# Adding the experts' down bias to the residual once, and moving the last tile's gates behind the first up projection

## The chip, the cores and the metric

The kernel runs on one core of a Trainium2 chip. The metric is the device time of one execution in microseconds (us). A core has a matrix engine (TensorE, "PE" in the profile, with its weight loads as "PEld"), a vector engine (VectorE, "DVE"), a scalar engine (ScalarE, "ACT"), GpSimd ("POOL") and SyncE ("SP"), which here only issues DMAs. Each engine works through its own queue in program order; semaphores join the queues. Sixteen DMA engines move data for all of them.

## The reference, cut to what matters

The kernel computes one decoder block for 512 tokens of width 1024: norm, two attention mixers, output projection, residual, and then a mixture of 32 experts of which each token takes four. Only the last part is touched. In the reference it is

```
logits = (xt @ router_w + router_b)
top_v, top_i = lax.top_k(logits, TOP_K)
gate = softmax(top_v)
...
hc = xb @ w1[e] + b1[e]
gt = minimum(hc[:, :D_FF], 7);  up = clip(hc[:, D_FF:], -7, 7)
glu = gt * sigmoid(1.702 * gt)
y = ((up + 1.0) * glu) @ w2[e] + b2[e]        # b2: the down bias
out[token] += gate * y                        # for the token's four experts
```

so that a token's share of the down biases is the sum over its four experts of gate times `b2[e]`: one product of the 512 x 32 matrix of gates with the 32 x 1024 matrix of biases.

## The kernel before

**Stages.** Until about 479 us the core computes norm, projections and attention. From 479 to 549 us the output projection runs in eight half tiles (four token tiles of 128 rows, `NT`, two halves of 512 columns); between them `add_x` adds each half to the residual `xs`, and the router works tile by tile: `choose` picks four experts, `shift`, an exponential on ScalarE and `weigh` make the gates (stored as three half-precision pieces in `value`), `place` and `mark` make one-hot matrices, and `fill_table` multiplies them into a table in PSUM banks 0 and 1. For each expert it has 96 slots (`CAP`) with token number and three gate pieces. The last tile's one-hots come in three parts (`HOT_PARTS`). `take_table` turns the token numbers into gather indices; `fill_gates` then adds the last tile's gate pieces to the same table, and `take_gates` joins them into slot gates (`row_of`), which `spread_rows` and `after_first` spread over 128 rows for the scatter. `after_first` also counts experts with more than 96 tokens (`many`, `extra`).

**Experts.** Expert `e` runs in `expert(e, ...)` and `second(e, ...)`. Weights come as 12 slabs of 1 MB: eight (`w1`) for the up projection and four (`w2`) for the down one, each with one place in the buffer `ring`. On TensorE the order is `up(e)`, `turn_x(e+1)` (transposes of the next gathered rows), `down(e-1)`, `turn_act(e)`, `up(e+1)`. `up` starts with four small bf16 matmuls that put the up bias (L1556), then eight slabs of 12 matmuls (L1562). `down` starts with eight bf16 matmuls that put the down bias into PSUM banks 4 and 5 (L1569, L1572), then four slabs (L1580, L1584). f32 matmuls leave two records each. The biases lie in `bias` as three bf16 pieces stacked over 96 rows; `split_bias` makes them. GpSimd copies one-hot columns for each expert (`picked` into `pick_up`, `pick_down`), gathers the expert's rows from the normed copy `table_d` in HBM two experts ahead (`gathered`), and adds the results to the residual copy `x2_d` in HBM (`scattered`, two indirect DMAs). `store_x2(t)` on SyncE writes `x2_d` first, one tile of 512 KB at a time.

**What sets the order.** Everything is written out by hand. SyncE loads a slab again as soon as TensorE has used it: `load_w1(e+1)` while `up(e)` runs, `load_w2(e)` while `down(e-1)` runs, each slab behind a wait on `w1_used` or `w2_used`. So the ring holds just one expert's weights, and a slab asked for when expert `e` frees its place is wanted again one expert later. The indirect DMAs go through another queue to the same 16 DMA engines.

## Time and profile before

| | |
|---|---|
| median of 3 runs | 1676.53 us (1675.32 to 1678.14) |
| the profiled execution | 1675.77 us |
| its span, first to last instruction | 1674.0 us |
| PE busy | 1591.8 us, 95% |
| DVE, ACT, POOL busy | 440.9, 259.8, 233.9 us |
| chain of work that ended last | PE 88%, DVE 5%, ACT 3%, issue 2%, DMA 1% |
| weight slabs (SyncE's queue) | 384 of 1 MB, median 19.8 us from issue to landing |
| bytes moved | 472.35 MB, 282 GB/s over the span |

Between the span and the run's own time lie 1.77 us. Read the table as the average of stages with different limits: up to 549 us DMA is lightly used, and from about 568 us to the end both TensorE and the 16 DMA engines show 90% or more in nearly every slice. The page gives the slices; the trace gives, for each DMA issue, the time to its landing, and that is the number to follow here.

### The profile page before, as it was taken

The numbers are of one execution on the slowest core, as the hardware profiler recorded it, in microseconds if no ns is written. First come the engines' busy times: TensorE is split into PE (matmuls) and PEld (weight loads), VectorE is DVE, ScalarE is ACT, GpSimd is POOL, SyncE is SP. The second block draws the span as 40 slices with busy tenths as digits, with TensorE's granted clock in tenths as the row PEclk, the third lists the DMA queues.
The fourth block names the chain that finished last, engine by engine and source line by source line (L and its number), as shares of the span: only waits on it lengthen the run. The fifth ranks groups of instructions, "written<-read, shape, count | busy, mean of one in ns | idle before, by whom it ended". The sixth has DMA issues, their size and how long they took to land.

```text
span 1674.0 us, 32752 instructions
## 1 busy us (share of the span) xinstructions
PE 1591.8 (95%) x13380; PEld 645.9 (39%) x13381; DVE 440.9 (26%) x966; ACT 259.8 (16%) x541; POOL 233.9 (14%) x377
## 2 busy tenths in 40 slices
PE   5999999999999789999999999999999999999992
PEld 2654555565445323333333333333333333333331
DVE  4012555332325422113111311131112111211222
ACT  3212444323322100000000000000000000000002
POOL 1000000522200101111111111111111111121101
PEclk8999999999999799999999999999999999999996
DMA  8023120431251789999999999999999999999995
GB/s 224 1 54 73 38 76 13 136 88 51 65 200 51 275 342 376 388 393 386 396 386 395 392 399 386 391 394 399 389 396 399 401 389 394 400 402 390 400 383 177
DMA packets 150302, 472.35 MB, mean 282 GB/s; under 512 B 30537, under 2 KB 71497, under 8 KB 117458
## 3 DMA queue, kind: packets, MB, share of 16 engines
q1 hardware_dynamic: 137458, 446.56, 69.1%
q0 software_dynamic: 12800, 25.17, 6.9%
q8 instruction: 31, 0.51, 0.1%
q14 instruction: 13, 0.11, 0.0%
HBM read 452.41 MB, written 19.29 MB: 282 GB/s over the span
## 4 chain that ended last, share of the span: by engine, by line
PE 88%; DVE 5%; ACT 3%; issue 2%; DMA 1%; DVEq 0%; PEld 0%; POOL 0%; ACTq 0%; PEldq 0%; POOLq 0%; SPq 0%
PE ps L1562 40%; PE ps L1580 13%; PE ps L1181 12%; PE ps L1584 7%; PE ps L1510 3%; PE ps L1323 3%; PE ps L1308 2%; PE ps L1595 2%; PE ps L1536 2%; ACT mixT L995 2%; PE ps L1285 1%; ACT mixT L1004 1%; PE ps L1295 1%; DVE ps L1797 1%; PE ps L1556 1%
## 5 line engine op out<-in xcount | busy, mean ns | idle before, releaser
L1562 PE MATMUL ps<-ring,oT_fox 128*32 128x512 f32 x6144 | 668.8, 595 | 0.0
L1562 PEld LDWEIGHTS ps<-ring,oT_fox 128*32 128x32 f32 x6144 | 184.1, 110 | 462.8 <-issue 459.2
L1580 PE MATMUL ps<-ring,hT 128*32 128x512 f32 x2048 | 264.1, 592 | 0.0
L2101 DVE TENSOR_TENSOR mixT<-ps,mask 128x768 f32<-128x768 f32 x64 | 61.1, 954 | 650.2 <-PE ps L1562 650.2
L1584 PE MATMUL ps<-ring,hT 128*32 128x256 f32 x2048 | 154.8, 379 | 0.0
L1323 PE MATMUL ps<-hT,ring 128*128 128x512 f32 x304 | 137.3, 599 | 0.0
L1584 PEld LDWEIGHTS ps<-ring,hT 128*32 128x32 f32 x2048 | 61.3, 110 | 158.4 <-issue 158.4
L1119 ACT ACTIVATE mixT<-mixT 128x768 f32<-128x768 f32 x32 | 27.0, 845 | 609.8 <-DVE mixT L2105 609.8
L1181 PE MATMUL ps<-hT,ring 128*128 128x512 f32 x208 | 93.2, 609 | 7.0 <-ACT hT L929 7.0
L841 POOL COPY pT<-pT 96x32 bf16 (+1 forms) x64 | 13.8, 218 | 575.5 <-ACT hT L1129 566.3
L2130 DVE COPY hT<-ps 128x384 f32<-128x384 f32 x64 | 32.8, 553 | 181.0 <-PE ps L1595 180.9
L1323 PEld LDWEIGHTS ps<-hT,ring 128*128 128x128 f32 x304 | 55.5, 191 | 64.2 <-issue 64.2
L1129 ACT ACTIVATE hT<-ps,v_fox 128x512 f32<-128x512 f32 x64 | 33.7, 577 | 295.9 <-PE ps L1584 295.9
L1580 PEld LDWEIGHTS ps<-ring,hT 128*32 128x32 f32 x2048 | 61.1, 110 | 46.5
L1181 PEld LDWEIGHTS ps<-hT,ring 128*128 128x128 f32 x208 | 40.2, 195 | 56.5 <-issue 56.4
L995 ACT ACTIVATE mixT<-ps,st 128x128 f32<-128x128 f32 (+1 forms) x96 | 49.1, 536 | 78.1 <-DVE st L1803 78.1
L1510 PE MATMUL ps<-ring,mixT 128*128 128x512 f32 x128 | 59.0, 601 | 2.1 <-DVE qk L1930 2.1
L832 POOL DMA_INDIRECT x<-hT,v_win x32 | 50.6, 1580 | 26.2 <-POOL v_win L829 24.5
L834 POOL DMA_INDIRECT x<-hT,v_win x32 | 49.7, 1552 | 9.8 <-issue 9.8
L1181 PEld LDWEIGHTS ps<-ring,hT 128*128 128x128 f32 x384 | 45.2, 192 | 2.3 <-issue 2.3
L1181 PE MATMUL ps<-ring,hT 128*128 128x128 f32 (+1 forms) x384 | 45.5, 279 | 0.0
L818 POOL COPY v_win<-v_win 96x1 int32 (+1 forms) x30 | 5.9, 196 | 259.4 <-DMA x<-hT,v_win 231.0
(291 smaller groups left out, 1162.4 us busy)
## 6 DMA issues: line engine op xcount, KB each, us to landing
ring<-in_expert_w SPq DMA_DIRECT2D x384, 1024.0 KB, 19.8
ring<-in_w_in SPq DMA_DIRECT2D x28, 512.0 KB, 4.8
ring<-in_w_out SPq DMA_DIRECT2D x8, 512.0 KB, 7.6
ring<-in_w_in SPq DMA_DIRECT2D x1, 3168.0 KB, 12.9
xs<-in_x SPq DMA_DIRECT2D x4, 512.0 KB, 5.1
ring<-in_w_in SPq DMA_DIRECT2D x8, 256.0 KB, 3.6
ring<-in_w_proj_nsa SPq DMA_DIRECT2D x16, 128.0 KB, 2.9
ring<-in_w_proj_fox SPq DMA_DIRECT2D x8, 256.0 KB, 3.3
```

The source lines that it names most:

```text
L832: pool.indirect_dma_start(out=x2_half, out_offset=bass.IndirectOffsetOnAxis(ap=now_half[b], axis=0), in_=yb[b][:, 0:512], in_offset=None, ...
L834: pool.indirect_dma_start(out=x2_quarter, out_offset=bass.IndirectOffsetOnAxis(ap=now_quarter[b], axis=0), in_=yb[b][:, 512:768], in_offse ...
L995: last = act.activation(probs[:, h, P_OFF[t]:P_OFF[t] + P * (t + 1)], scores(h, t), ACT.Exp, bias=ngm[:, h, t:t + 1], accum_out=sums[:, h, ...
L1129: ins = act.activation(yb[b][:, cols], y_ps[:, cols], ACT.Copy, scale=gate)
L1181: last = pe.matmul(dst, lhs(c), rhs(c), start=(c == 0), stop=(c == n - 1))
L1308: ins = pe.matmul(o_bank[h * DH:(h + 1) * DH, kt * P:S], v[:, kt, h * DH:(h + 1) * DH], pT[:, h, at:at + S - kt * P], start=(first and n = ...
L1323: ins = pe.matmul(w, w_c(c), hT[:, c, :], start=(c == 0), stop=(c == NK - 1))
L1510: ins = pe.matmul(ps[:, u, :], mixT[:, k, t * P:(t + 1) * P], w_o[k][:, n * 512:(n + 1) * 512], start=(k == 0), stop=(k == NK - 1))
L1562: ins = pe.matmul(wide(ps[TG * j:TG * j + TG, g, :]), xT[b][:, c, TG * g:TG * g + TG], up_slab(c, j), start=(c == 0), stop=(c == NK - 1), ...
L1580: pe.matmul(ps[TG * q:TG * q + TG, 4, :], gT[b][:, 2 * (q // 2) + h, TG * j:TG * j + TG], ring[:, NK + j, at:at + 512], start=False, stop= ...
L1584: ins = pe.matmul(ps[TG * q:TG * q + TG, 5, 0:256], gT[b][:, 4 + h, TG * j:TG * j + TG], ring[:, NK + j, at:at + 256], start=False, stop=( ...
L2101: return dve.tensor_tensor(to, half, b_up[:, 256 * n:256 * n + 256].unsqueeze(1).broadcast_to([P, NG, 256]), ALU.add)
```

## The change

- The down bias leaves the experts. `down` puts none; `pick_down` and its copies on GpSimd go, and `split_bias` makes pieces of the up bias alone.
- In its place the biases are loaded as f32 into `rope_cos` and `rope_sin`, four copies of 32 rows each (eight DMAs of 64 KB, issued before the projection of the mixers). `give_b_down(k)`, for k from 0 to 3, multiplies transposed gates by them, two matmuls of 32 rows by 128 columns over 512 columns each, after the slabs 4 to 7 of `up(1)`; VectorE adds each 128 x 512 result to `xs`, eight additions.
- `xs` is complete only then. The four `x2_d` stores move from the router's stage (three there, one after the first gather) to SyncE's queue between `load_w1(2)` and `load_w2(1)`. GpSimd's wait for them stands where it stood, ahead of `block(1)`; `down(0)` waits for the last addition, since banks 4 and 5 hold the products.
- `fill_gates` writes to a part of bank 5 of its own and runs after `turn_x(1)`, inside `expert(0)`, with four matmuls more that transpose the gates and one that clears. `take_gates` and `after_first` come after `expert(0)` on VectorE, `spread_rows` after slab 2 of `up(1)`; the count of overfull experts (`count_extra`) comes ahead of `expert(0)`. `take_parts` saves the table.

```diff
@@ b_raw, b_mid, bias, pick_up
-        b_raw = [ring_f[0:E, 0:2 * F], hT_f[0:E, 0:D]]
+        b_raw = ring_f[0:E, 0:2 * F]
+        b_down = [rope_cos, rope_sin]
+        gates_T = pcT[:, 0:P]
@@ SyncE
-            sp.dma_start(b_raw[1], expert_b2[0]).then_inc(b_loaded, 16)
+            for n in range(2):
+                for t in range(NT):
+                    sp.dma_start(b_down[n][E * t:E * (t + 1), :], expert_b2[0][:, n * 512:(n + 1) * 512]).then_inc(b_loaded, 16)
...
             for t in range(NT - 1):
-                store_x2(t)
                 store_table(t)
...
             sp.wait_ge(xg_loaded[0], 16)
-            store_x2(NT - 1)
...
             load_w1(1)
-            with sp.Fori(1, E - 1) as e:
+            load_w1(2)
+            sp.wait_ge(x2_ready, 4 * NT)
+            for t in range(NT):
+                sp.dma_start(x2_d[1 + t * P:1 + (t + 1) * P, :], xs[:, t, :]).then_inc(x2_stored, 16)
+            load_w2(1)
+            with sp.Fori(2, E - 1) as e:
@@ GpSimd
             picked(pick_up, 0, 0, pick_up_ready)
-            for b in range(2):
-                picked(pick_down, b, b, pick_down_ready)
-            pool.wait_ge(idx_ready, 6)
+            pool.wait_ge(idx_ready, 2)
...
             block(0, 0, True, 0)
             pool.wait_ge(x2_stored, 16 * (NT + 1))
+            pool.wait_ge(idx_ready, 6)
@@ TensorE
             def fill_gates():
                 pe.wait_ge(gates_ready, NT)
+                for t in range(NT):
+                    pe.matmul(ps[E * t:E * (t + 1), 4, 0:P], expd[:, t, :], ident[:, :], start=True, stop=True,
+                              tile_position=(0, E * t))
...
-            pe.wait_ge(idx_ready, 2)
-            fill_gates()
...
             def down(b, loaded, used):
-                for q in range(4):
-                    n = q % 2
-                    pe.matmul(ps[TG * q:TG * q + TG, 4, :], pick_down[:, b, :], bias[:, 2 * F + n * 512:2 * F + (n + 1) * 512],
-                              start=True, stop=False, tile_position=(0, TG * q))
-                for q in range(4):
-                    pe.matmul(ps[TG * q:TG * q + TG, 5, 0:256], pick_down[:, b, :], bias[:, 2 * F + q * 256:2 * F + (q + 1) * 256],
-                              start=True, stop=False, tile_position=(0, TG * q))
...
+            def give_b_down(k):
+                if k == 0:
+                    pe.wait_ge(idx_ready, 6)
+                    pe.wait_ge(b_loaded, 16 * (2 * NT + 1))
+                else:
+                    pe.wait_ge(x2_ready, 2 * NT + 2 * k)
+                for m in range(2):
+                    t = 2 * (k % 2) + m
+                    rows = slice(E * t, E * (t + 1))
+                    pe.matmul(ps[:, 4 + m, :], gates_T[rows, :], b_down[k // 2][rows, :], start=True, stop=True,
+                              tile_position=(E * t, 0)).then_inc(b_down_full, 1)
...
+                    if isinstance(e, int) and e == 1 and c >= 4:
+                        give_b_down(c - 4)
+                    if isinstance(e, int) and e == 1 and c == 2:
+                        pe.wait_ge(rows_ready, 1)
+                        spread_rows(4, 0, 2 * E, row_of.rearrange("p v e -> p (v e)")).then_inc(table_full, 1)
...
+                if not before:
+                    fill_gates()
...
-                pe.wait_ge(pick_down_ready, e + 1)
+                else:
+                    pe.wait_ge(x2_ready, 4 * NT)
@@ VectorE
+                for k in range(4):
+                    for m in range(2):
+                        t, n = 2 * (k % 2) + m, k // 2
+                        dve.wait_ge(b_down_full, 2 * k + m + 1)
+                        sl = xs[:, t, n * 512:(n + 1) * 512]
+                        dve.tensor_tensor(sl, sl, ps[:, 4 + m, :], ALU.add).then_inc(x2_ready, 1)
...
             take_x(0, 0)
+            count_extra()
+            expert(0, 0, True)
+            take_gates()
             after_first()
-            expert(0, 0, True)
```

SyncE's queue after the last tile's table store (`table<-hT`; `x<-xs` is a store to `x2_d`, `ring<-in_expert_w` a slab, 2x1024 wide for `w2`). Before:

```order
L615 DMA table<-hT 128x1024 [waits x_normed]
L619 DMA x<-xs 128x1024 [waits x2_ready,xg_loaded0]
L611 DMA ring<-in_expert_w 128x2x1024 x4
L611 DMA ring<-in_expert_w 128x2048 [waits w1_used] x8
L650 UNCONDITIONAL_BRANCH
```

and changed:

```order
L622 DMA table<-hT 128x1024 [waits x_normed]
L618 DMA ring<-in_expert_w 128x2x1024 [waits xg_loaded0]
L618 DMA ring<-in_expert_w 128x2x1024 x3
L618 DMA ring<-in_expert_w 128x2048 [waits w1_used] x16
L654 DMA x<-xs 128x1024 [waits x2_ready]
L654 DMA x<-xs 128x1024 x3
L618 DMA ring<-in_expert_w 128x2x1024 [waits w2_used] x4
L656 UNCONDITIONAL_BRANCH
```

All four stores now stand behind the slabs that `up(1)` frees and ahead of those that `down(0)` frees.

TensorE from the last one-hot part to the first slab of expert 0 (`ident,oT_nsa` is `turn_x`, `v_fox,ident` is `spread_rows`, `pT` the up bias). Before:

```order
L1495 MATMUL ps<-v_sel,qk 96x3 [waits gates_ready,idx_ready]
L1495 MATMUL ps<-v_sel,qk 96x3 x31
L1536 MATMUL ps<-ident,oT_nsa 128x96 [waits rows_ready,xg_loaded0,consts2,bias_ready]
L1536 MATMUL ps<-ident,oT_nsa 128x96 x7
L1503 MATMUL ps<-v_fox,ident 32x64 x8
L1556 MATMUL ps<-pT 32x512 [waits pick_up_ready,xT_ready]
L1556 MATMUL ps<-pT 32x512 x3
L1562 MATMUL ps<-ring,oT_fox 32x512 [waits slab_loaded0]
```

and changed:

```order
L1538 MATMUL ps<-ident,oT_nsa 128x96 [waits idx_ready,xg_loaded0,consts2,bias_ready]
L1538 MATMUL ps<-ident,oT_nsa 128x96 x7
L1558 MATMUL ps<-pT 32x512 [waits parts_taken,pick_up_ready,xT_ready]
L1558 MATMUL ps<-pT 32x512 x3
L1564 MATMUL ps<-ring,oT_fox 32x512 [waits slab_loaded0]
```

`turn_x(0)` no longer waits for `rows_ready`; the gather (`xg_loaded0`) stays.

TensorE from slab 6 of `up(1)` to `down(0)` (`rope_sin,pcT` is `give_b_down`). Before:

```order
L1562 MATMUL ps<-ring,oT_fox 32x512 [waits slab_loaded6]
L1562 MATMUL ps<-ring,oT_fox 32x512 x11
L1562 MATMUL ps<-ring,oT_fox 32x512 [waits slab_loaded7]
L1562 MATMUL ps<-ring,oT_fox 32x512 x11
L1536 MATMUL ps<-ident,oT_nsa 128x96 [waits gT_ready,xg_loaded0]
L1536 MATMUL ps<-ident,oT_nsa 128x96 x7
L1569 MATMUL ps<-pT 32x512 [waits pick_down_ready,gT_ready]
L1569 MATMUL ps<-pT 32x512 x3
L1572 MATMUL ps<-pT 32x256 x4
L1580 MATMUL ps<-ring,hT 32x512 [waits slab_loaded8]
```

and changed:

```order
L1564 MATMUL ps<-ring,oT_fox 32x512 [waits slab_loaded6]
L1564 MATMUL ps<-ring,oT_fox 32x512 x11
L1607 MATMUL ps<-rope_sin,pcT 128x512 [waits x2_ready]
L1607 MATMUL ps<-rope_sin,pcT 128x512
L1564 MATMUL ps<-ring,oT_fox 32x512 [waits slab_loaded7]
L1564 MATMUL ps<-ring,oT_fox 32x512 x11
L1607 MATMUL ps<-rope_sin,pcT 128x512 [waits x2_ready]
L1607 MATMUL ps<-rope_sin,pcT 128x512
L1538 MATMUL ps<-ident,oT_nsa 128x96 [waits gT_ready,xg_loaded0]
L1538 MATMUL ps<-ident,oT_nsa 128x96 x7
L1575 MATMUL ps<-ring,hT 32x512 [waits slab_loaded8,x2_ready,gT_ready]
```

The eight bias matmuls at the head of `down` are gone, for this and every other expert; pairs of new ones stand between the slabs of `up(1)` alone, and `down(0)` waits for the additions.

## Rows read from the trace of the kernel before

**Rows 1.** TensorE's timeline over one expert: start, length (us), line, count.

```profile
668.18 20.77 PE L1562 MATMUL ps<-ring,oT_fox 128*32 128x512 f32 x192
...
689.70 0.40 PE L1569 MATMUL ps<-pT 96*32 96x512 bf16 x4
...
690.03 1.03 PE L1580 MATMUL ps<-ring,hT 128*32 128x512 f32 x8
...
701.49 20.77 PE L1562 MATMUL ps<-ring,oT_fox 128*32 128x512 f32 x192
```

**Rows 2.** Slab loads, five singly, then all: issue (ns), start and landing (us).

```profile
L611 SPq DMA_DIRECT2D ring<-in_expert_w x1: 333/333/333, 622.6 to 622.6; - x1
...
DMA to landing us min/median/max: 6.1/6.1/6.1
...
L611 SPq DMA_DIRECT2D ring<-in_expert_w x1: 349/349/349, 637.9 to 637.9; - x1
...
DMA to landing us min/median/max: 7.9/7.9/7.9
...
L611 SPq DMA_DIRECT2D ring<-in_expert_w x1: 4060/4060/4060, 1137.5 to 1137.5; - x1
...
DMA to landing us min/median/max: 22.9/22.9/22.9
...
L611 SPq DMA_DIRECT2D ring<-in_expert_w x1: 3864/3864/3864, 1544.2 to 1544.2; - x1
...
DMA to landing us min/median/max: 21.5/21.5/21.5
...
L611 SPq DMA_DIRECT2D ring<-in_expert_w x1: 3457/3457/3457, 1554.7 to 1554.7; - x1
...
  PEld ps L1562: 0.3, 1
...
DMA to landing us min/median/max: 27.8/27.8/27.8
...
DMA to landing us min/median/max: 4.8/19.8/29.9
```

**Rows 3.** Stretches: us, busy time by engine, PE clock, DMA share, GB/s.

```profile
494.50:498.80 4.30, 4.30 (x14) 2.10 (x13) 1.51 (x6) 2.42 (x4) 0.58 (x1) 1.00 0.30 122
600.00:604.00 4.00, 4.00 (x24) 0.85 (x20) 0.00 (x0) 0.00 (x0) 0.00 (x0) 0.56 0.17 58
624.00:640.00 16.00, 16.00 (x186) 5.68 (x178) 5.37 (x9) 2.50 (x4) 3.64 (x5) 1.00 0.95 342
```

**Rows 4.** DMA queues, 1360 to 1460 us: packets, MB, share of 16 engines.

```profile
q1 hardware_dynamic: 6647, 37.26, 92.2%
q0 software_dynamic: 1200, 2.36, 10.6%
```

**Rows 5.** Timeline of all engines from the last residual addition to `turn_x(0)`.

```profile
548.71 0.69 DVE L1943 TENSOR_TENSOR xs<-xs,ps 128x512 f32<-128x512 f32 x1 [3.74 <-PE ps L1510]
...
561.62 2.69 PE L1495 MATMUL ps<-v_sel,qk 128*96 128x3 f16 x32 [0.96 <-DVE v_win L2007]
563.41 0.33 SPq L619 DMA_DIRECT2D x<-xs  x1
...
566.09 1.51 PE L1536 MATMUL ps<-ident,oT_nsa 96*128 96x96 f32 x8 [1.78 <-DVE v_fox L2011]
```

**Rows 6.** Timeline of all engines between the first two up projections.

```profile
592.58 0.61 POOL L818 COPY v_win<-v_win 96x1 int32 x1 [21.37 <-PE ps L1536]
...
594.93 0.23 POOL L841 COPY pT<-pT 96x32 bf16 x1
...
597.78 1.51 PE L1595 MATMUL ps<-ident,mixT 128*128 128x128 f32 x6 [5.46 <-DVE mixT L2127]
...
599.62 22.72 PE L1562 MATMUL ps<-ring,oT_fox 128*32 128x512 f32 x192
```

**Rows 7.** The score matmuls' (L1285) own busy time in a stretch.

```profile
167.00:169.60 2.60, 2.43 (x16) 1.69 (x16) 1.00 0.00 0
```

More of the change, by code:

```diff
@@ L437, in hybrid_block @@
         rows_ready = sem("rows_ready")
+        parts_taken = sem("parts_taken")
         bias_hi = sem("bias_hi")
@@ L1584, in down @@
                         ins = pe.matmul(ps[TG * q:TG * q + TG, 5, 0:256], gT[b][:, 4 + h, TG * j:TG * j + TG],
-                                        ring[:, NK + j, at:at + 256], start=False, stop=(c == NK - 1),
+                                        ring[:, NK + j, at:at + 256], start=(c == 0), stop=(c == NK - 1),
                                         tile_position=(0, TG * q))
@@ L2016, in valid_row, with take_parts @@
                 yield dve.tensor_tensor(to, pad, v, ALU.add)
+            def take_parts():
+                step.link(dve.tensor_copy(split[:, HOT_PARTS[0][1]:, :], table_of(HOT_PARTS[0][1], E)))
+                step.link(dve.tensor_copy(split[:, 0:HOT_PARTS[0][1], :], table_of(0, HOT_PARTS[0][1])))
+                dve.sem_inc(parts_taken, 1)
             def take_gates():
                 dve.wait_ge(table_full, NT + 3)
-                for first, end in ((0, HOT_PARTS[0][1]), (HOT_PARTS[0][1], E)):
-                    step.link(dve.tensor_copy(split[:, first:end, :], table_of(first, end)))
+                step.link(dve.tensor_copy(gates_T, ps[:, 4, 0:P]))
+                step.link(dve.tensor_tensor(split[:, :, 1:4], split[:, :, 1:4], late_of(0, E), ALU.add))
                 for ins in valid_row(row_of[:, 0, :], split[:, :, 0], row_pad):
@@ L2055, in _ @@
             step.link(dve.tensor_copy(count, routed(NT - 1, 2)))
+            take_table(1)
+            take_parts()
             weigh(NT - 1)
-            take_table(1)
-            take_gates()
             def slot_rows(to_half, to_quarter, halves_, quarters_, signal):
```

74 lines of the change are left out of this document (34 added, 40 removed).

## The prediction

> **What bounds the kernel now.** I read the slices of the page first: from about 568 us on TensorE is busy and its clock is full, so a TensorE-bound kernel is the first guess. Its timeline over one expert confirms the pace [rows 1]: `up(3)` begins at 668.18 and `up(4)` at 701.49, 33.31 us apart, and an up projection takes 20.77 us, 2.6 us for a slab. No wait stands between.
>
> But DMA is as busy. In 100 us of this stretch the slab loads take 92.2% of the 16 engines and the indirect DMAs 10.6% [rows 4]: full, at 37.26 + 2.36 MB or 396 GB/s. Whether DMA keeps up is told by the time from issue to landing [rows 2]. The slab asked for at 637.9 (the first of expert 3) lands after 7.9 us, the same slab of expert 18, asked for at 1137.5, after 22.9, and the last but one of expert 30's up slabs, asked for at 1554.7, after 27.8. So a queue builds up: TensorE asks for 12 slabs in 33.31 us, and DMA delivers them in more. From landing to landing, expert 3 to 18: (1160.4 - 645.8) / 15 = 34.31 us. Expert 18 to 30 (1544.2 + 21.5 = 1565.7): (1565.7 - 1160.4) / 12 = 33.78 us. A ring of one expert's weights can lend about 30 us, and it has lent them all: at 1554.7 + 27.8 = 1582.5 a weight load of TensorE waited 0.3 us for exactly that slab [rows 2]. TensorE reached its matmuls at 1567.5 (668.18 plus 27 periods) + 6 x 2.59 = 1583.0. So the slack, wide at first, ends at about 0.5 us just before the end. **The kernel before is TensorE-bound by half a microsecond, with DMA behind it.** What TensorE saves is worth at most that, until the last slabs of expert 30 have come; what DMA is given to carry is what to count.
>
> **What TensorE saves and pays.** (a) The head of `down`: from 689.70 to 690.03 the matmuls of the down bias hold it for 0.34 us [rows 1] (their records are longer but overlap). 32 x 0.34 = 10.9 us go, with nothing beside them on TensorE. (b) The start of expert 0: `turn_x(0)` begins at 566.09, after `fill_gates` (561.62, 2.69 us) and VectorE's `take_gates` [rows 5]. Without them the gather is late next: SyncE, which waits for it too, goes on at 563.41. So it can begin near 563.45, 2.6 us earlier, and not more. `take_parts` and `weigh` on VectorE, some 2.7 us after the last one-hot, are done before the transposes are. (c) `fill_gates` goes into a hole: between `turn_x(1)` and `turn_act(0)` TensorE is idle for 5.46 us [rows 6], while VectorE and ScalarE work on expert 0. It took 2.69 us at half clock, and with five matmuls more stays under 4 at either clock, so it costs nothing. (d) Of the clock: from 599.62 `up(1)` takes 22.72 us instead of 20.77, since the clock fell to 1.2 GHz in the hole (mean 0.56 between 600 and 604, [rows 3]). With the hole half filled the clock either stays at 2.4 GHz, 2.0 us gained, or falls again, nothing gained; I call it even.
> (e) Inside `up(1)`: the spread is 8 small f32 matmuls, nearest to the eight turning ones (1.51 us at half clock, [rows 5]), 0.4 at least, 0.8 at most at full. The eight matmuls of `give_b_down` have 512 columns of f32. Twelve of up's, four abreast, take 2.59 us, so one alone takes 0.86. A pair uses different rows of the array. The score matmuls, two heads on 64 rows each, show what that does: 8 matmuls with 2560 columns, 4.3 us one after the other, take 2.43 us [rows 7]. So a pair takes 0.86 to 1.73 us; I take 0.97, since only the scores have this form: four pairs 3.9 us (3.5 to 6.9). The waits in them are covered: two additions of 0.69 us [rows 5] lie under the 2.6 us of the next slab. After the last pair they are not: 1.5 us, of which `turn_x(2)` covers 0.8, leaves 0.7 before `down(0)`.
> The chapter on packing small matmuls in the Trainium skill (TensorE: Matmul & The Clock Gate, Part 3) states that tiles on different row groups run concurrently and that four with 32 rows gained 3.07 times; by it a pair would cost 0.9, which the scores' row supports for two groups.
>
> TensorE alone would thus end 10.9 + 2.6 - 0.4 - 3.9 - 0.7 = 8.5 us earlier, 10.5 with the clock kept.
>
> **What DMA is given.** (f) The four stores to `x2_d` were spread over the router's stage, where DMA is a third busy: one store, alone between 494.5 and 498.8, is 0.30 of 4.3 us, 1.3 us of all 16 engines [rows 3]. Now they are issued near 623 us, four times 1.3 = 5.2 us. (g) GpSimd waits for them ahead of `block(1)`. Behind that wait stand the gather for expert 3, the pick of expert 2's up bias and the first scatter. The gather ran near 594 [rows 6], and DMA was at 0.17 from 600 to 604 [rows 3]; now it comes after 631. The indirect DMAs of an expert cost 10.6 / 3 = 3.5 us [rows 4], a gather between a third and a half: 1.2 (to 1.8). (h) What the queue can use: from 624 to 640 DMA was at 0.95, 0.8 us idle [rows 3]. (i) When the queue starts. Since it stands nearly still at 600, it starts when `up(1)` frees its first slab. That is 2.6 us earlier from (b), 4.6 with the clock kept; the spread and three pairs delay the last slab by 3.3. So that slab, asked for at 622.6 and landed at 628.7 [rows 2], is asked for at 621.3. With 3.6 us from one slab to the next no queue is left then, and it lands after the least that any load took, 4.8 us [rows 2]: at 626.1, 2.6 us earlier than before, or 0.6 if the clock falls. The stores follow within 2.5 us of its request, so DMA does not stand still between.
> Sum of f to i at `w1(3)`: 5.2 + 1.2 - 0.8 - 2.6 = **3.0 us later** (5.0 if the clock falls). `up(2)` starts as before or 2 us later.
>
> **From there to the end.** TensorE's period is now 33.31 - 0.34 = 32.97, and the landing time grows by 34.31 - 32.97 = 1.34 us an expert, from 7.9 + 3.0 = 10.9 at expert 3. There is one thing to gain. DMA was faster, 33.78 instead of 34.31, from the point on at which a slab took 22.9 us to land; there an issue, before 0.35 us long, took SyncE 4.06 us [rows 2], so the queue was full. If the rate goes with the full queue (what the rows suggest and do not prove), it comes after (22.9 - 10.9) / 1.34 = 9 experts, at 12 instead of 18: 6 x 0.53 = 3.2 us gained. Slab 6 of expert 30 then lands -0.2 us (clock kept) to +1.8 us against before. TensorE, up to some 8 us early, will have run into the queue near expert 20 and takes it at landing. The end, against the profiled execution: the slack of 0.5 goes, and three `down`s after it are shorter by 1.0: -1.5 - 0.2 = -1.7 us, or -1.5 + 1.8 = +0.3. The middle is -0.7 us on 1675.77: 1675.1. The median of the runs is 0.76 above that execution, so 1675.8 us.
> The pages DMA: Bandwidth & Descriptors (Bandwidth) and HBM Reference (Specifications) of the Trainium skill give 425 GB/s for a core streaming alone. At that rate an expert's data would take 31 us, DMA would stay ahead and the first rival below would hold; the 396 GB/s of rows 4, with all engines occupied, speak against it for this mix of loads and scatters.
>
> **Rivals.**
> *TensorE's gain arrives.* If DMA speeds up under more pressure, as it did once by 1.5%, to 33 us an expert, the end follows TensorE: 1675.77 - 8.5 or - 10.5, on the median 1666 to 1668. It needs 0.8 us an expert more than any stretch showed. 0.1.
> *No quickening.* The faster rate belongs to something else (the late experts' addresses, say) and does not come sooner: +3.2, on the median 1678.0 with the clock kept, 1680.0 without. 0.28.
> *Slower: the stores and the gather in the full queue.* The stores and the gather are simply more for a full queue: without quickening, with the clock falling, a pair at 1.73 (three of them, +2.3 before the last slab is freed) and a gather at 1.8, it is 5.0 + 2.3 + 0.6 - 1.5 = +6.4, on the median 1683. It is slower by over 0.2% from the point at which slab 6 of expert 30 lands 4.9 us later than before. 0.1, beside the slow end of the case above.
> *A stall from the stores.* `up(2)` needs its pick, 2.6 us after GpSimd's wait ends (592.58 to 595.16, [rows 6]). The stores land near 631, the pick comes at 633.6, `up(2)` starts at 668.18 - 33.31 = 634.9. If it is late by 1 or 2 us, TensorE has 20 us of slack in hand at that place: no effect on the end.
> *It does not do what it says* is excluded for the matmuls, which are gone from the program's order.
>
> **How the numbers follow.** The likeliest, DMA-bound with the faster rate sooner, has 0.5 and gives 1675.8, its own range 1673.0 to 1678.5. No quickening 0.28, TensorE's gain 0.1, slower beyond it 0.1, and 0.02 left over. A measurement of this kernel tells 0.2%, 3.4 us, from no change: below 1673.2 is faster, above 1679.9 slower. Faster: 0.1 from the first rival and 0.11 of the likeliest. Same: 0.39 of the likeliest and 0.18 of no quickening. Slower: 0.1 of that, 0.1, and the rest. The range leaves out the gain and the worst of the slower side: 1671 to 1681.
>
> **What the changed profile will show if this is right.** The period of TensorE 32.97 us until about expert 20, then waits of PEld for `ring<-in_expert_w` in nearly every expert, together some 8 us, and a period of 33.7. Slabs near expert 12 landing after 23 us, SyncE's issues getting long from there on rather than from expert 18. `turn_x(0)` at 563.5, `down(0)` near 623.4, stores issued at 623 and landed by 632. Wrong, if no wait for slabs shows (then the first rival), if the landing time starts above 12 us at expert 3 (then the traffic was under-counted), or if the rate near expert 15 is still 34.3.

## The result, and the profile after

The changed kernel takes 1679.01 us (median of 20 runs, 1676.28 to 1681.70) against 1676.64 us (1674.34 to 1678.44, 20 runs): a ratio of 1.0015, with a 95% interval of 1.0009 to 1.0021. It is **slower by 2.4 us** where 0.7 us faster was forecast. It stays inside the stated range of 1671 to 1681 us, but the sign was wrong. Measured once more (e15 below), it gave 1.0014 (1.0005 to 1.0023).

The chain of work that ended last, by engine, now holds 21% of DMA, where before it was 1%:

```profile
PE 68%; DMA 21%; DVE 5%; ACT 3%; issue 2%; DVEq 0%; PEld 0%; SPq 0%; POOL 0%; ACTq 0%; PEldq 0%; POOLq 0%
```

TensorE's timeline over one expert, which answers to rows 1 (start, length in us, line, count):

```profile
672.07 20.77 PE L1564 MATMUL ps<-ring,oT_fox 128*32 128x512 f32 x192
692.78 0.88 PE L1538 MATMUL ps<-ident,oT_nsa 96*128 96x96 f32 x8
693.59 1.07 PE L1575 MATMUL ps<-ring,hT 128*32 128x512 f32 x8
...
705.08 7.47 PE L1564 MATMUL ps<-ring,oT_fox 128*32 128x512 f32 x68
```

The down bias is gone and the period is 705.08 - 672.07 = 33.0 us, as predicted (32.97). The slab loads, which answer to rows 2: slab 7 of expert 2, slab 0 of experts 3 and 12, slab 6 of expert 30 (issue in ns, start, time to landing in us), then who waited for any slab from 1200 us on:

```profile
L618 SPq DMA_DIRECT2D ring<-in_expert_w x1: 328/328/328, 625.1 to 625.1; - x1
...
DMA to landing us min/median/max: 4.7/4.7/4.7
...
L618 SPq DMA_DIRECT2D ring<-in_expert_w x1: 356/356/356, 642.0 to 642.0; - x1
...
DMA to landing us min/median/max: 11.1/11.1/11.1
...
L618 SPq DMA_DIRECT2D ring<-in_expert_w x1: 3186/3186/3186, 939.1 to 939.1; - x1
...
DMA to landing us min/median/max: 22.9/22.9/22.9
...
L618 SPq DMA_DIRECT2D ring<-in_expert_w x1: 953/953/953, 1560.8 to 1560.8; - x1
...
  PEld ps L1564: 0.7, 1
...
DMA to landing us min/median/max: 26.0/26.0/26.0
...
  PEld ps L1564: 19.8, 33
```

Slab 0 of expert 3 lands at 653.1, 7.3 us later than before (645.8, [rows 2]). It took 11.1 us to land, where the sum gave 10.9, but that this fits is luck: it was asked for 4.2 us later and landed 7.3 us later, both more than forecast. At expert 12 a slab takes 22.9 us and the issue 3.2 us, the state that the kernel before reached at expert 18. From about expert 20 TensorE's weight loads wait for slabs (33 waits in up alone; most of each lies beside matmuls that still run, and the period is 33.8). Slab 6 of expert 30 lands at 1586.8 instead of 1582.5. So the course of the queue (the loads asked for and not yet landed) is the one foretold; its start is later than foretold. Where that start is set, in TensorE's timeline of `up(1)` (answers to rows 6):

```profile
596.99 1.51 PE L1590 MATMUL ps<-ident,mixT 128*128 128x128 f32 x6 [3.52 <-DVE mixT L2158]
...
598.83 7.34 PE L1564 MATMUL ps<-ring,oT_fox 128*32 128x512 f32 x52
```

```profile
608.15 0.39 PE L1507 MATMUL ps<-v_fox,ident 96*32 96x64 f32 x16
608.38 5.32 PE L1564 MATMUL ps<-ring,oT_fox 128*32 128x512 f32 x48
613.63 1.13 PE L1607 MATMUL ps<-rope_cos,pcT 32*128 32x512 f32 x4
614.69 2.78 PE L1564 MATMUL ps<-ring,oT_fox 128*32 128x512 f32 x24
617.40 1.13 PE L1607 MATMUL ps<-rope_cos,pcT 32*128 32x512 f32 x4
...
627.48 1.06 PE L1575 MATMUL ps<-ring,hT 128*32 128x512 f32 x8 [0.61 <-issue]
```

A pair holds the slabs up by 617.40 - 613.63 - 2.59 = 1.18 us, the spread by 0.23, and `down(0)` waits 0.6 us for the last additions. The DMA engines before (first fence) and after (second), in stretches: us, busy time by engine, granted clock, DMA share, GB/s:

```profile
600.00:610.00 10.00, 10.00 (x80) 2.45 (x76) 0.00 (x0) 0.60 (x1) 0.00 (x0) 0.82 0.51 181
610.00:620.00 10.00, 10.00 (x96) 2.62 (x92) 0.00 (x0) 0.00 (x0) 0.00 (x0) 1.00 1.00 407
620.00:624.00 4.00, 4.00 (x48) 1.62 (x44) 1.44 (x3) 0.00 (x0) 0.00 (x0) 1.00 1.01 412
```

```profile
600.00:604.00 4.00, 4.00 (x32) 0.94 (x28) 0.53 (x3) 0.60 (x1) 0.00 (x0) 0.75 0.08 33
...
600.00:610.00 10.00, 10.00 (x100) 2.64 (x96) 1.13 (x7) 0.60 (x1) 0.00 (x0) 0.90 0.59 224
610.00:620.00 10.00, 10.00 (x84) 2.62 (x80) 2.57 (x4) 0.00 (x0) 0.00 (x0) 1.00 0.92 354
620.00:624.00 4.00, 4.00 (x36) 1.01 (x32) 1.28 (x2) 0.00 (x0) 0.00 (x0) 1.00 0.73 285
624.00:628.00 4.00, 3.39 (x32) 1.37 (x28) 1.90 (x3) 0.00 (x0) 0.00 (x0) 1.00 0.76 291
...
624.00:640.00 16.00, 15.37 (x174) 7.15 (x170) 8.00 (x12) 1.90 (x3) 1.65 (x5) 1.00 0.95 359
```

With a slab freed every 3.77 us DMA runs dry between slabs just where the kernel before keeps it full. From 624 to 640 us it is at 0.95, as before ([rows 3]): the 0.8 us of idle time there, which the stores were to use, is idle still. And the hole before `turn_act(0)` is still 3.5 us wide, and the clock fell in it as before.

### The profile page after: what moved, and what is told of

Its sections match the earlier page's. It is cut to its first block, busy times and chain, and to the rows that moved or that the text cites. A ratio compares the mean times of both kernels' runs of the same rounds, so it can differ in the third digit from the quotient of the medians.

```text
span 1677.1 us, 32232 instructions
## 1 busy us (share of the span) xinstructions
PE 1588.6 (95%) x13149; PEld 649.4 (39%) x13150; DVE 444.1 (26%) x974; ACT 255.8 (15%) x537; POOL 229.8 (14%) x345
## 4 chain that ended last, share of the span: by engine, by line
PE 68%; DMA 21%; DVE 5%; ACT 3%; issue 2%; DVEq 0%; PEld 0%; SPq 0%; POOL 0%; ACTq 0%; PEldq 0%; POOLq 0%
PE ps L1564 26%; DMA ring<-in_expert_w 20%; PE ps L1180 11%; PE ps L1575 10%; PE ps L1579 5%; PE ps L1514 3%; PE ps L1322 3%; PE ps L1307 2%; ACT mixT L998 1%; PE ps L1284 1%; ACT mixT L1007 1%; PE ps L1294 1%; PE ps L1590 1%; PE ps L1538 1%; DVE ps L1817 1%
## 5 line engine op out<-in xcount | busy, mean ns | idle before, releaser
L1575 PE MATMUL ps<-ring,hT 128*32 128x512 f32 x2048 | 267.7, 594 | 7.3 <-DMA ring<-in_expert_w 5.7
L1579 PEld LDWEIGHTS ps<-ring,hT 128*32 128x32 f32 x2048 | 67.0, 110 | 152.7 <-issue 152.7
L835 POOL COPY v_win<-v_win 128x1 int32 (+1 forms) x64 | 9.7, 183 | 554.2 <-ACT hT L1128 554.2
L1575 PEld LDWEIGHTS ps<-ring,hT 128*32 128x32 f32 x2048 | 61.4, 109 | 54.5 <-DMA ring<-in_expert_w 16.0
L1128 ACT ACTIVATE hT<-ps,v_fox 128x512 f32<-128x512 f32 x64 | 33.6, 577 | 295.0 <-PE ps L1579 295.0
```

Of the source, the lines that this page charges most:

```text
L1128: ins = act.activation(yb[b][:, cols], y_ps[:, cols], ACT.Copy, scale=gate)
L1575: pe.matmul(ps[TG * q:TG * q + TG, 4, :], gT[b][:, 2 * (q // 2) + h, TG * j:TG * j + TG], ring[:, NK + j, at:at + 512], start=(c == 0), st ...
L1579: ins = pe.matmul(ps[TG * q:TG * q + TG, 5, 0:256], gT[b][:, 4 + h, TG * j:TG * j + TG], ring[:, NK + j, at:at + 256], start=(c == 0), sto ...
```

## The experiments

Each run was measured beside the kernel before, on the same chip. "Against before" is the ratio of the times; 0.001 is 1.7 us, and gains in the text are differences of these ratios. e1, e5, e6 and e14 leave the down bias out of the output, and e3 and e4 part of the down weights: they are there to price a part. The times to the right are of the profiled execution: start of `up(0)`, `up(1)` and `up(2)`, slab 7 of expert 2 asked for, slab 0 of expert 3 landed, and from there to the landing of slab 0 of expert 30 (us; "-": the trace has no landings of weight slabs there).

| run | median | against before (95%) | up(0) | up(1) | up(2) | 2.7 asked | 3.0 landed | to 30.0 |
|---|---|---|---|---|---|---|---|---|
| before | 1676.64 | 1 | 568.7 | 599.6 | 634.9 | 622.6 | 645.8 | 919.9 |
| change | 1679.01 | 1.0015 (1.0009-1.0021) | 568.6 | 598.8 | 639.1 | 625.1 | 653.1 | 917.1 |
| e15, change again | 1679.77 | 1.0014 (1.0005-1.0023) | 568.7 | 599.8 | 640.9 | 626.4 | 655.2 | 917.4 |
| e1, stores early | 1676.14 | 0.9999 (0.9991-1.0008) | 567.3 | 597.9 | 638.3 | 624.4 | 647.5 | 918.4 |
| e2, before, late stores | 1683.40 | 1.0043 (1.0030-1.0055) | 570.8 | 600.8 | 639.1 | 623.2 | 652.3 | 923.0 |
| e3, change, 11 MB | 1670.98 | 0.9968 (0.9955-0.9981) | 569.3 | 600.3 | 641.1 | 626.9 | 652.0 | 889.7 |
| e4, before, 11 MB | 1676.32 | 0.9998 (0.9989-1.0007) | 571.5 | 601.4 | 636.1 | 623.8 | 647.3 | 897.7 |
| e5, before, no bias | 1673.66 | 0.9978 (0.9968-0.9988) | 571.1 | 601.9 | 636.7 | 624.7 | 647.9 | 918.4 |
| e6, no pairs | 1678.02 | 1.0011 (1.0002-1.0020) | 567.8 | 599.1 | 639.2 | 622.4 | 652.3 | 918.8 |
| e7, gather first | 1678.23 | 1.0009 (1.0000-1.0018) | 568.0 | 599.3 | 640.0 | 626.1 | 652.3 | 917.9 |
| e14, no pairs, pick first | 1674.52 | 0.9987 (0.9978-0.9996) | 567.8 | 599.0 | 634.3 | 622.2 | 649.9 | 916.2 |
| e13, late stores, pick first | 1678.29 | 1.0013 (1.0004-1.0021) | 570.3 | 600.1 | 634.8 | 622.3 | 650.0 | 917.9 |
| e9, hole filled | 1676.43 | 0.9995 (0.9986-1.0004) | 569.0 | 599.3 | 638.0 | 624.0 | 653.7 | 914.2 |
| e12, before, hole filled | 1674.04 | 0.9985 (0.9976-0.9994) | 570.5 | 599.5 | 632.8 | 620.5 | - | - |
| e8, bias in up(0) | 1673.06 | 0.9977 (0.9968-0.9986) | 569.5 | 603.2 | 637.2 | 625.0 | - | - |
| e10, change, clock kept | 1673.05 | 0.9982 (0.9973-0.9991) | 567.9 | 596.0 | 634.5 | 620.6 | - | - |
| e11, up(0), clock kept | 1669.55 | 0.9955 (0.9942-0.9969) | 569.5 | 600.2 | 633.4 | 621.2 | - | - |

**What is the saving worth alone, and to TensorE alone?** e5 is the kernel before with the eight bias matmuls of `down` (L1569, L1572) deleted. e3 and e4 take DMA out of the way, in the change and in before:

```diff
                     dst = ring[:, c, :].rearrange("p (k n) -> p k n", k=2)
+                    if c >= 10 and not (isinstance(e, int) and e == 0):
+                        dst, src = dst[:, 0, :], src[:, 0, :]
```

> The kernel before without the eight down bias matmuls at the head of down, for all experts; nothing else of the change (the down bias is missing from the output). It does the gain of the change alone, with no traffic moved and no pairs. Theory T1 (DMA ends it): TensorE's period falls to 32.97 us but the end follows DMA: the queue fills some 4 experts earlier (18 to about 14), which gives 1.5 to 2 us, 0.7 us come from down(0) and down(1) at the start and 1.0 us from the last three downs: 2.5 to 3.5 us faster than before. Rival (TensorE's saving arrives whole): 32 x 0.34 = 10.9 us faster. Rival (the rate quickens at a fixed expert, whatever the queue): 1 to 1.5 us faster.

> The changed kernel, but for experts 1 to 31 half of each of the last two down slabs is not loaded (11 MB an expert instead of 12, so the output is wrong from expert 1 on); TensorE does the same work. This takes DMA out of the way and shows what the change is worth to TensorE alone. T1: no queue builds up, TensorE's period is 32.97 us to the end, and the end is 6.5 to 8.5 us ahead of the kernel before. Rival T3 (TensorE's saving is not there, for instance because the down bias was hidden beside the slabs): within 1 us of the run with the same loads on the kernel before.

> The kernel before with the same halves of down slabs left out from expert 1 on (output wrong in the same way). If the kernel before is bound by TensorE with 0.5 us to spare, as read, it keeps its time: 0 to 0.7 us less. If DMA already costs it something through contention or through late slabs that the trace does not show, it gains more than 1 us.

The saving alone gives 3.7 us, a little more than the 2.5 to 3.5 expected and far from 10.9: DMA ends it, as held. e4 keeps its time (0.3 us less, inside its interval), so the kernel before is bound by TensorE; in e3 all 27 experts take 889.7 us from landing to landing, 32.95 each, and it ends 5.3 us ahead of e4. That is TensorE's gain from the whole change: 5.3 (medians; 5.0 by the ratios), not the 8.5 that I summed. `up(2)` begins 5.0 us later in e3 than in e4 although `up(0)` begins 2.2 us earlier. So 3 us of the sum were wrong on TensorE's own side, all before `up(2)`.

**The stores.** e1 puts them back, e2 moves them in the kernel before:

```diff
@@ e1, SyncE (the additions on VectorE wait for x2_stored)
             for t in range(NT - 1):
+                store_x2(t)
                 store_table(t)
...
             sp.wait_ge(xg_loaded[0], 16)
+            store_x2(NT - 1)
...
             load_w1(2)
-            sp.wait_ge(x2_ready, 4 * NT)
-            for t in range(NT):
-                sp.dma_start(x2_d[1 + t * P:1 + (t + 1) * P, :], xs[:, t, :]).then_inc(x2_stored, 16)
@@ e2, SyncE
-                store_x2(t)
                 store_table(t)
...
             sp.wait_ge(xg_loaded[0], 16)
-            store_x2(NT - 1)
...
             load_w1(1)
-            with sp.Fori(1, E - 1) as e:
+            load_w1(2)
+            sp.wait_ge(x2_ready, 2 * NT)
+            for t in range(NT):
+                sp.dma_start(x2_d[1 + t * P:1 + (t + 1) * P, :], xs[:, t, :]).then_inc(x2_stored, 16)
+            load_w2(1)
+            with sp.Fori(2, E - 1) as e:
```

> The changed kernel with the four x2_d stores put back to the router's stage, where they stood before. The additions of the down bias come after them, so the down bias is missing from the output; all else runs as in the changed kernel. Theory T1 (the DMA traffic that the change puts into the full queue decides): slab 0 of expert 3 lands 5 to 7 us earlier than with the change (653.1 there), near 647; the rate then quickens some 4 experts later, which gives back 2 to 2.5 us; the end is 2 to 4 us earlier than with the change, 0 to 1.5 us ahead of the kernel before. Rival T2 (what TensorE does and waits for inside the first two up projections decides: pairs, spread, clock): the same time as the change, 2 to 2.5 us behind the kernel before, and slab 0 of expert 3 within 1.5 us of 653.

> The kernel before with one thing of the change alone: the four x2_d stores moved to SyncE's queue between load_w1(2) and load_w2(1). Down bias and gates stay as they were. T1: slab 0 of expert 3 lands 5 to 6 us later than before (645.8), the quickening comes 4 to 5 experts earlier and gives back 2 to 2.5 us, and the slack of 0.5 us goes: 2 to 3 us slower than before. T2: no difference to before over 0.5 us.

e1 is 2.7 us faster than the change (ratios 0.9999 and 1.0015) and its slab lands at 647.5, as theory T1 has it. e2 has the traffic (652.3) but costs 7 us, more than twice what T1 gave. Its waits of TensorE from 635 to 642 us and its timeline show why (GpSimd's copy that sat idle for the stores, its pick, `up(2)`):

```profile
PE ps L1555 <- POOL pT L840: 3.2, 1, 3.2
```

```profile
636.42 0.18 POOL L817 COPY v_win<-v_win 96x1 int32 x1 [63.09 <-DMA x<-xs]
...
638.34 0.37 POOL L840 COPY pT<-pT 96x32 bf16 x2
...
638.71 0.62 PE L1555 MATMUL ps<-pT 96*32 96x512 bf16 x4 [3.24 <-POOL pT L840]
```

Its clock in three stretches from there on was at 0.74, 0.50 and 0.90:

```profile
636.00:640.00 4.00, 1.29 (x12) 0.46 (x16) 0.20 (x1) 0.00 (x0) 1.94 (x7) 0.74 1.03 422
640.00:644.00 4.00, 4.00 (x24) 0.97 (x20) 0.00 (x0) 0.00 (x0) 2.97 (x2) 0.50 1.02 353
644.00:648.00 4.00, 4.00 (x40) 1.16 (x36) 0.00 (x0) 0.60 (x1) 0.00 (x0) 0.90 1.11 306
```

The stores land late in the queue, the pick of expert 2 stands behind them on GpSimd, TensorE waits 3.2 us, the clock falls, and `up(3)` begins at 675.2 (668.1 in e13, without the stall). This is the stall that the prediction priced at nothing. e13 is e2 with one line of GpSimd moved:

```diff
                     picked(pick_down, e + 1, o, pick_down_ready)
+                    pool.wait_ge(x2_stored, 16 * (NT + 1))
                     now_scatter(e - 1, o)
...
             block(0, 0, True, 0)
-            pool.wait_ge(x2_stored, 16 * (NT + 1))
```

> The kernel before with the late stores (as in the second run of the first set, which was 6.7 us slower than before), and with GpSimd's gather for expert 3 and its picks for expert 2 ahead of the wait for these stores. Output complete. Theory (the stores cost twice there: 2 MB in a full queue, and up(2), whose pick stood behind GpSimd's wait for them, 3.2 us late and then 6.8 us at 1.2 GHz): up(2) starts on time, the clock stays, up(3) begins 5 to 6 us earlier than in that run, and what is left is the traffic: 2 to 3.5 us slower than before. Rival (it is all traffic, the stall is hidden by slack): 5.5 to 7 us slower than before, as without this edit.

1.0013 instead of 1.0043: 5 us were the stall, 2.2 us the traffic. In the change itself `up(2)` just escapes: the pick was there at 638.70 and the first matmul at 638.84; in e15 TensorE waited 0.5 us for it.

**The gather** (the same move of GpSimd's wait in the change, e7):

> The changed kernel with GpSimd's gather for expert 3 and its pick for expert 2 ahead of the wait for the x2_d stores instead of behind it (output complete). T1: the gather runs near 594 us, when DMA is nearly idle, instead of in the full queue: slab 0 of expert 3 lands 1.2 us earlier, of which the later quickening takes 0.4 back: 0.5 to 1.2 us faster than the change. If up(2) waits for that pick (it came 0.14 us before up(2)'s first matmul in the changed kernel), some executions gain 1 to 3 us more and the spread of the times becomes smaller. Rival: the gather costs nothing there, same time within 0.3 us.

1.0 us by the ratios, inside the expectation and not separable from zero by the intervals; the slab lands 0.8 us and 2.9 us earlier than in the two profiles of the change.

**The pairs.** e6 is the change without `give_b_down` and without the additions; e14 is e6 with GpSimd's move of e7.

```diff
-                    if isinstance(e, int) and e == 1 and c >= 4:
-                        give_b_down(c - 4)
+                    if isinstance(e, int) and e == 1 and c == 4:
+                        pe.wait_ge(idx_ready, 6)
```

> The changed kernel without the eight matmuls of give_b_down and the eight additions (the down bias is missing from the output); the stores stay behind load_w1(2). Three pairs stand before the last slab that up(1) frees. If a pair costs 1.18 us there, as the slab periods of the changed kernel show (3.77 against 2.59 us), slab 7 of expert 2 is asked for 3.5 us earlier, slab 0 of expert 3 lands 3 to 4 us earlier (near 649.5), the quickening comes 2 to 3 experts later and gives 1.2 to 1.6 us back: 1.5 to 2.5 us faster than the change. Rival (the traffic alone counts, when TensorE frees a slab does not, since a queue stands anyway): within 0.5 us of the change.

> The changed kernel without the pairs and additions (down bias missing from the output), with GpSimd's gather for expert 3 and pick for expert 2 ahead of the wait for the stores. Against the run with the gather first and the pairs in place (1.2 us slower than before) it tells what the pairs cost without the stall of up(2) that spoiled the earlier run without pairs. Theory: without pairs DMA is not idle between the slabs of up(1) (0.6 MB, 1.5 us) : 1 to 2 us faster than that run, within 0.7 us of before. Rival (the pairs cost TensorE 5 us, and TensorE's position counts): 3.5 to 5 us faster than that run. Rival (nothing of the pairs reaches the end): within 0.4 us of it.

e6 gained only 0.7 us, and it decides nothing: with TensorE earlier, `up(2)` waited 4.4 us for its pick.

```profile
PE ps L1558 <- POOL pT L847: 4.4, 1, 4.4
```

Without that stall (e14) the pairs' absence gives 3.7 us against e7, which is the rival's number and twice mine. `up(1)` to `up(2)` takes 35.3 us in e14 and 40.7 in e7: the pairs and the wait behind them cost TensorE 5.4 us, not 4.6. And without them DMA is kept full from 610 to 624 us:

```profile
610.00:620.00 10.00, 10.00 (x100) 2.61 (x96) 0.00 (x0) 0.00 (x0) 0.00 (x0) 1.00 0.98 396
620.00:624.00 4.00, 4.00 (x44) 1.52 (x40) 1.69 (x3) 0.14 (x1) 0.00 (x0) 1.00 1.05 397
```

That is 396 and 397 GB/s, against 354 and 285 in the change. I had expected 1.5 us from the idle DMA and the later quickening to take part of it back. It took nothing: e14 asks for slab 0 of expert 3 at 637.3, 5.7 us earlier than e7, and gets it only 2.4 us earlier, so its queue is the deeper one (12.6 us to landing against 9.3) and the faster rate comes sooner, not later. e14 takes away two things at once, the idle DMA and TensorE's 5.4 us; what each of them costs at the end is not separated.

**The clock.** Five matmuls that nobody reads fill the hole before `turn_act(0)` in the change (e9), seven in the kernel before (e12):

```diff
                 if not before:
                     fill_gates()
+                    pe.wait_ge(b_loaded, 16 * (2 * NT + 1))
+                    for _ in range(5):
+                        pe.matmul(ps[:, 4, P:4 * P], ident[:, :], b_down[0][:, P:4 * P], start=True, stop=True)
```

> The changed kernel with five more f32 matmuls of 384 columns (3.2 us at full clock) right behind fill_gates, into a part of bank 4 that nobody reads; the output is complete. They fill the hole before turn_act(0) that the change left 3.5 us wide. Theory: TensorE is then without a pause of more than 0.5 us there, the granted clock stays at 2.4 GHz from 571 us on instead of falling near 595 for 6.8 us, up(1) takes 2.0 us less in the stretch 598 to 602, and the end is 1.0 to 2.0 us ahead of the change. Rival: the clock falls whatever stands in the hole: 0 to 0.5 us slower than the change. If DMA sets when slab 0 of expert 3 lands whatever TensorE's clock does, up(1) is 2 us shorter and the end stays.

> The kernel before with seven such matmuls of 384 columns (into bank 5, read by nobody) between turn_x(1) and turn_act(0), where TensorE is idle for 5.5 us. Output complete. It tells what the clock's fall at 596.7 us costs a kernel that TensorE bounds: the fall gone, up(1) 1.7 to 2.0 us shorter, all slabs from expert 2 on asked for 2 us earlier; the slack at expert 30 stays as it is, and the end is 1.5 to 2.0 us faster than before. Rival (DMA sets the end whatever TensorE does from here): 0 to 0.5 us faster.

The stretch from 594 to 604 us in the change, then in e9 (granted clock third from the end):

```profile
594.00:604.00 10.00, 7.01 (x46) 2.60 (x50) 5.25 (x12) 0.60 (x1) 0.00 (x0) 0.66 0.60 247
```

```profile
594.00:604.00 10.00, 9.81 (x82) 4.53 (x84) 6.30 (x14) 1.15 (x2) 0.00 (x0) 1.00 0.70 270
```

A mean of 0.66 is 6.8 of 10 us at 1.2 GHz. The clock fell there in each of the seven profiles with the change's hole and in each of the six with a wider or similar one, and in none of the four with such matmuls. e9 is 3.3 us faster than the change, e12 2.5 us faster than before; `up(1)` to `up(2)` takes 38.7 us in e9, where the change had 40.2 and e15, with its wait of 0.5 us, 41.2; and 33.3 in e12 instead of 35.3. Each gives somewhat more than the 1.6 to 2.0 us of the stretch, and more than I expected. In e9 that is a faster queue (914.2 us to expert 30, slab 0 of expert 3 no earlier), which I can't explain fully.
The page TensorE: Matmul & The Clock Gate (Why this matters for your kernels) of the Trainium skill says that idle gaps between bursts of matmuls are to be avoided, because the clock drops back after them; e9 and e12 agree, with 1.00 from 594 to 604 us where the change and the kernel before had 0.66.

**A version that beats both.** e8 computes the same as the change with the product in `up(0)`, four matmuls on four row groups at once after slabs 3 and 5, the stores between `load_w1(1)` and `load_w1(2)`, and the gather first. e10 is e7 with matmuls in TensorE's waits at the hole and between 554 us and `turn_x(0)`; e11 is e8 with those.

```diff
@@ e8, TensorE (up(0)) and SyncE
+                    if not before and c == 1:
+                        turn_gates()
+                    if not before and c in (3, 5):
+                        give_b_down((c - 3) // 2)
...
             load_w1(1)
-            load_w1(2)
             sp.wait_ge(x2_ready, 4 * NT)
             for t in range(NT):
                 sp.dma_start(x2_d[1 + t * P:1 + (t + 1) * P, :], xs[:, t, :]).then_inc(x2_stored, 16)
+            load_w1(2)
@@ e10 and e11, TensorE (keep_busy: as many f32 matmuls of 384 columns)
             route(2 * NT - 1)
+            pe.wait_ge(b_loaded, 16 * (2 * NT + 1))
+            keep_busy(3)
             count_earlier(NT - 1)
             for part in range(len(HOT_PARTS)):
+                if part < 2:
+                    keep_busy(1 + part)
                 fill_table(NT - 1, part)
+            keep_busy(4)
```

> The same computation as the changed kernel, with the same removals from down, but what the change puts into up(1) stands in up(0): the gates are transposed after slab 1, and after slabs 3 and 5 four matmuls of give_b_down on four row groups at once; VectorE adds during up(0); the four x2_d stores go between load_w1(1) and load_w1(2), and GpSimd's gather for expert 3 ahead of its wait for them. Theory (two things made the change slower: the stores in a full queue, and the pairs that leave DMA idle between the slabs of up(1)): the stores fill the hole that DMA has at 600 to 606 us (share 0.17 to 0.6), up(1) has no pairs, slab 0 of expert 3 lands within 1.5 us of where the kernel before has it (645.8 to 647.3), and the end is 0 to 2.5 us faster than before, 2.5 to 5 us faster than the change. If only the stores counted: as the run with the stores early, 0 to 0.5 us faster than before. If the product of gates and biases costs DMA or TensorE the same wherever it stands: within 1 us of the change.

> The changed kernel with the gather first and with matmuls that nobody reads (128 x 128 by 384 columns of f32) in TensorE's waits: five behind fill_gates as before, and ten between the last router matmuls at 554 us and turn_x(0). Output complete. Theory (at the two places the clock falls because TensorE waits, and it costs up(0) and up(1) at 1.2 GHz): the granted clock stays at 2.4 GHz from the output projection to the last expert; up(0) begins 0.5 to 1.5 us earlier and takes 1.5 to 2.5 us less, up(1) 2 us less; all slabs are asked for 4 us earlier, of which the later quickening takes 1 to 1.5 back: 3.5 to 6 us faster than the change, 1 to 4 us faster than before. Rival (the clock falls there whatever TensorE does): 0.5 to 3 us faster than the change, from the hole alone.

> The kernel with the down bias in up(0) and the stores behind load_w1(1), with the same matmuls in TensorE's waits as the run above. Output complete. If the two causes (traffic and idle DMA on one side, the clock on the other) add up, it is 3 to 6 us faster than before; if what one gives is taken back by the queue's later quickening, 2 to 3 us.

e8 gives 0.9977, 3.9 us faster than before and more than expected: as much as the saving alone (e5, 0.9978), so the rest of the change (the earlier `up(0)` on one side, product, stores and gates on the other) comes to nothing at the end. Which of e8's edits does it, the product's place, its four row groups, the stores' place or the gather, is not separated. From 600 to 604 us its DMA engines are full with the stores, where those of the change had 0.08 ([rows 3] had 0.17):

```profile
600.00:604.00 4.00, 2.65 (x14) 1.49 (x18) 2.76 (x7) 0.00 (x0) 0.00 (x0) 0.50 1.00 411
```

e10 gives 0.9982, 5.5 us less than the change, as expected, and e11 0.9955: **7.5 us faster than before** (7.1 by the medians), more than expected. The two causes add up nearly: the extra matmuls give 4.5 us on e7 (e10) and 3.7 us on e8 (e11). In e10 the clock stood at 0.89 from 556 to 572 us, where the change had 0.52, and from `up(0)` to `up(1)` it took 28.0 us instead of 30.2:

```profile
594.00:604.00 10.00, 9.81 (x105) 3.39 (x107) 3.18 (x9) 0.60 (x1) 0.00 (x0) 1.00 1.01 371
556.00:572.00 16.00, 13.76 (x106) 7.04 (x110) 11.58 (x32) 1.46 (x3) 5.04 (x6) 0.89 0.67 242
```

The trace of e11 has TensorE waiting for slabs as often as that of the change (34 times in `up`, 36 in the change), so DMA still ends it.

**The change again.**

> The changed kernel once more, unedited, for a second profiled execution. In the first one all of TensorE's work up to 556 us came 2.6 us late because of where the clock had fallen early in the execution. If that was chance, this execution has another lead or lag there (up(0) from 566 to 569.5 us), and what lies between up(0) and slab 0 of expert 3 (84.5 us in the first) is the same within 1 us; the median is 2 to 3 us above the kernel before.

The median is 2.4 to 2.8 us above before both times. `up(0)` begins at 568.6 and 568.7. The kernels with the start of before begin it at 570.3 to 571.5, except the profiled execution of before itself, at 568.7: that one was ahead of its kind by some 2 us, not the change behind by 2.6. From `up(0)` to the landing it was 84.5 and 86.5 us, 2 us apart where I expected 1, so the last 1 or 2 us of a sum made from single traces are chance.

## Why the prediction was wrong, step by step

Means of profiled executions: of the runs with the start and `up(1)` of before (before, e2, e4, e5, e13) and of those with the start and pairs of the change (the change twice, e1, e3, e7).

- **(a), and what bounds the kernel before: right.** Period 33.0; e4 shows TensorE as the limit, e5 DMA close behind it. The half microsecond itself is read from one trace, and both fit it.
- **(b), half wrong.** `up(0)` begins 568.4 instead of 570.5, 2.1 us earlier (2.6 predicted; the gather was late next, as said: `turn_x(0)` waited 2.8 us for it). But `up(1)` begins only 1.5 us earlier (599.2, 600.8). The time won lies in a stretch at 1.2 GHz, which ended at 572.3 us instead of 573.3, only about 1 us earlier: the same work took 30.8 us instead of 30.3.
- **(c), right:** `fill_gates` is hidden. **(d), the step that failed first.** I called the clock even and took the middle. It fell in all seven profiles that have this hole, in which 3.5 us without a matmul were left. That alone is 1.0 us of the forecast, and the case with the clock falling stood at +0.3. With the clock kept (e9) the sum stood at -1.7, and e9 measured -0.8 (-2.3 to +0.7). So the clock was worth 3.3 us at the end, where the sum had 2.0.
- **(e), mis-sized.** A pair 1.18 us instead of 0.97, additions as said, spread 0.23. Over `up(1)` to `up(2)` the change adds 5.7 us (40.6, 35.0; e2 with its stall left out, e5 counted with the 0.34 us that it saves) where the sum gave 4.7.
- **(f), (g), right:** stores 6.7 us between e1 and the mean of the change, 1.3 of it e1's earlier start, so 5.4 (5.2 predicted); the gather about 1 (1.2 predicted). **(h), wrong:** the 0.8 us of idle DMA from 624 to 640 us were not used, the share there is 0.95 as before, 0.93 in e15. From the landing of slab 7 of expert 2 to that of slab 0 of expert 3 the change takes 6.7 us more (23.4, 16.7), where f, g and h gave 5.6.
- **(i), the term that turned the sign.** Slab 7 of expert 2 was to be asked for 1.3 us earlier, or 0.7 later with the clock falling. It was 2.5 us later (625.8, 623.3): (b), (d) and (e) all come together here, since it is TensorE that frees the slab and DMA is idle until it does. It landed 0.4 us later than before (630.8, 630.3), not 2.6 or 0.6 us earlier; that it lands 4.8 us after it is asked for held (4.7 and 5.3 us). So the sum at slab 0 of expert 3 was +3.0 or +5.0 and the two profiles have 654.2 against 647.0 (before, e4, e5): **+7.2**.
- **The quickening, right.** A slab took 22.9 us to land at expert 12, as forecast. From slab 0 of expert 3 to that of expert 30 the change took 917.1 and 917.4 us, before 919.9: 2.7 us gained (3.2 predicted). With the prediction's 34.31 us an expert up to the point at which a slab takes 22.9 us, and 33.78 after it, the same rule gives 918.2 for e5 (measured 918.4), 918.7 for e1 (918.4), 917.9 for e13 (917.9) and 915.7 for e14 (916.2). It misses e2 (919.7 against 923.0) and e9 (916.2 against 914.2). The rule holds for sums, but it is no clean step: in the change the experts up to 13 come at 33.9 to 34.2 us, but three of them at 34.7 to 35.2, and 33.8 is reached at expert 14; in e13 the issues take 2.7 to 6.9 us from expert 12 on and the rate is 34.0 until expert 18. "No quickening" falls: an expert settled near 33.8 us (33.6 to 34.0) from expert 19 on in the kernel before, from 14 on in the change and from 13 on in e14, so the faster rate does not belong to fixed experts.
- **The end.** +7.2 - 2.7 - 1.5 = +3.0 us; the medians say +2.4 and +2.8. What bounds the kernel, and the quickening, held; the error is the 2.2 to 4.2 us at the queue's start: 1.0 to 3.0 of it at slab 7 of expert 2, by (b), (d) and (e), and 1.1 behind it, most of it (h).
- **The stall, priced at nothing, was wrong in its reason.** "20 us of slack in hand" is the time that a slab waits for TensorE, not time that TensorE can lose: a kernel bound by TensorE with 0.5 us to spare pays every stall (e2, e6). In the change it missed by 0.1 us, and in e15 TensorE waited 0.5 us.

## What to carry to other kernels

When two engines are nearly level, sum a change at the point where the second one's queue begins, and ask there when each buffer is freed: work put between the last buffers freed left DMA idle here, while the same work one stage earlier, where the loader is ahead, cost nothing at the end (e8). A fall of the clock belongs into the sum wherever a wait like those of this case is left (3.2 us in e2, 3.5 in the change, 4.4 in e6, 5.5 before); filling the wait with matmuls is worth trying even on an engine that is short of time. Move a wait on one engine only after looking at what small steps stand behind it in its queue.

## What was not expected of the hardware

A pair of f32 matmuls with 32 rows and 512 columns on two row groups took 1.06 us between two slabs (613.63 to 614.69), and four on four row groups took 1.07 us in e8:

```profile
582.31 1.14 PE L1604 MATMUL ps<-rope_cos,pcT 32*128 32x512 f32 x8
583.38 5.36 PE L1562 MATMUL ps<-ring,oT_fox 128*32 128x512 f32 x48
588.66 1.14 PE L1604 MATMUL ps<-rope_sin,pcT 32*128 32x512 f32 x8
```

Counted by what the slabs beside them were held up, it is 1.18 us for the pair and 1.17 for the four (588.66 - 582.31 - 2 x 2.59 in e8). So two more row groups were free, while a pair costs more than the 0.86 us that I estimated for a single one. Part 3 of the page TensorE: Matmul & The Clock Gate of the Trainium skill has matmuls on different row groups run at the same time, and the two numbers agree. I priced a pair by interpolation and did not ask what four would cost. And the loads ran 1.5% faster (33.8 us an expert instead of 34.3) some experts after SyncE's issues had become 2 us long and more, in every kernel with all its weights whose landing times I have: one expert later in the kernel before, three in the change, seven in e13. What about the full queue does that, no run here tells.
